# A two-block transformer kernel in fp32: raw first units, norm sums on TensorE, a shared convolution and new expert ends

## The reference

```
x = x + rms(conformer_conv(rms(x)*g));  x = x + rms(conv_ffn(rms(x)*g))   # first block
kv = rms(x) @ w_kv
x = x + rms(dilated_attention(rms(x)*g, kv)); x = x + rms(conv_ffn(...))  # second block
x = x + g1 * token_mixer(...)                 # mLSTM and differential attention
x = x + g2 * moe(...)                         # 32 experts, top 4 per token
return rms(x) * final_g
```

## Time and profile before

| | |
|---|---|
| median of 3 runs | 2433.94 us (2433.86, 2433.94, 2438.98) |
| profiled execution | 2438.93 us, span of the trace 2437.1 us |
| mean granted TensorE clock | 0.989 of full |
| busy: PE, DVE, ACT | 2360.7 (97%), 776.6 (32%), 424.8 us (17%) |
| read from HBM | 604.65 MB, 249 GB/s over the span |
| 192 expert loads | 2048 KB each, about 25 us from issue to landing |

### The profile page before, as it was taken

How to read it: one execution, slowest core, us unless ns; L and a number is a source line. 1 busy time by engine, 2 the same in 40 slices (tenths; PEclk the granted TensorE clock), 3 DMA queues, 4 the chain that set the end, 5 groups by cost and what they waited for, 6 DMA issues and landing times.

```text
span 2437.1 us, 31815 instructions
## 1 busy us (share of the span) xinstructions
PE 2360.7 (97%) x13140; PEld 1775.1 (73%) x13140; DVE 776.6 (32%) x1891; ACT 424.8 (17%) x1025; POOL 0.2 (0%) x4
## 2 busy tenths in 40 slices
PE   8899999999999999999999999999999999999997
PEld 7678887888888888988877787555555555555554
DVE  6843374310345422000344833222221111211122
ACT  3142202010142211100023502111111111111111
POOL 0000000000000000000000000000000000000000
PEclk9899999999999999899999999999999999999999
DMA  6124466665323443122122266999999999999995
GB/s 247 49 104 156 155 257 243 237 230 189 105 87 138 156 156 121 70 105 103 69 87 87 88 267 244 411 427 429 428 428 428 428 429 428 428 428 428 428 428 237
DMA packets 56631, 606.95 MB, mean 249 GB/s; under 512 B 6304, under 2 KB 6688, under 8 KB 7488
## 3 DMA queue, kind: packets, MB, share of 16 engines
q1 hardware_dynamic: 56544, 605.72, 62.1%
HBM read 604.65 MB, written 1.05 MB: 249 GB/s over the span
## 4 chain that ended last, share of the span: by engine, by line
PE 85%; DMA 7%; DVE 6%; issue 1%; ACT 1%; SPq 0%; DVEq 0%; ACTq 0%
PE bank L569 28%; PE bank L1067 17%; PE bank L566 8%; DMA ring<-in_experts 7%; PE bank L1093 6%; PE bank L632 5%; PE bank L583 3%; PE bank L1060 3%; PE bank L558 2%; DVE arena L1625 2%; PE bank L1028 2%; PE bank L1040 2%; PE bank L735 1%; PE bank L643 1%; PE bank L663 1%
## 5 line engine op out<-in xcount | busy, mean ns | idle before, releaser
L569 PE MATMUL bank<-arena,ring 128*128 128x256 f32 x3296 | 717.7, 380 | 0.0
L569 PEld LDWEIGHTS bank<-arena,ring 128*128 128x128 f32 x3296 | 627.6, 191 | 85.6
L2030 DVE TENSOR_SCALAR arena<-bank 128x256 f32<-128x256 f32 x64 | 27.2, 425 | 668.7 <-PE bank L1067 668.7
L1067 PE MATMUL bank<-ring,arena 128*64 128x256 f32 x2048 | 235.1, 382 | 4.8 <-DMA ring<-in_experts 4.8
L1067 PE MATMUL bank<-arena 128*64 128x256 f32 x2048 | 235.1, 382 | 2.1 <-DMA arena<-in_experts 2.1
L1067 PEld LDWEIGHTS bank<-ring,arena 128*64 128x64 f32 x2048 | 141.4, 137 | 91.3 <-issue 17.9
L1067 PEld LDWEIGHTS bank<-arena 128*64 128x64 f32 x2048 | 141.3, 137 | 88.4 <-issue 18.6
L566 PE MATMUL bank<-ring,arena 128*128 128x256 f32 x896 | 196.2, 381 | 0.0
L566 PEld LDWEIGHTS bank<-ring,arena 128*128 128x128 f32 x896 | 171.3, 191 | 23.5
L632 PE MATMUL bank<-arena,ring 128*128 128x256 f32 x576 | 124.6, 379 | 0.0
L632 PEld LDWEIGHTS bank<-arena,ring 128*128 128x128 f32 x576 | 109.4, 190 | 14.9
(11 more groups left out here) (270 smaller groups left out, 1959.4 us busy)
## 6 DMA issues: line engine op xcount, KB each, us to landing
arena<-in_experts SPq DMA_DIRECT2D x96, 2048.0 KB, 24.9
ring<-in_experts SPq DMA_DIRECT2D x96, 2048.0 KB, 26.5
ring<-in_dense SPq DMA_DIRECT2D x186, 1024.0 KB, 4.8
con<-in_con SPq DMA_DIRECT2D x1, 1248.0 KB, 12.2
X<-in_x SPq DMA_DIRECT2D x1, 1024.0 KB, 4.8
arena<-in_cond SPq DMA_DIRECT2D x1, 1024.0 KB, 17.6
arena<-in_ctx SPq DMA_DIRECT2D x1, 1024.0 KB, 4.8
arena<-in_mmask SPq DMA_DIRECT2D x1, 1024.0 KB, 6.8
```

What stands on the lines that cost most here:

```text
L569: ins = nc.tensor.matmul(o, w[:, k, j * P:(j + 1) * P], src[:, k, :], start=(k == 0), stop=(k == KT - 1))
L1067: ins = nc.tensor.matmul(o, XGT[:, k, e * CAP:(e + 1) * CAP], w[:, k, :], start=False, stop=(k == KT - 1), skip_group_check=True)
```

## The change

- **First two units.** ScalarE writes XG, X times the gain alone (in U's place), and units 0 and 1 multiply XG. The squares come after it; the sum (`presummed`) stands inside unit 0, before chunk 5. VectorE multiplies both halves of the two units by the factor as it reads PSUM (`raw_unit`), ScalarE takes the sigmoid in SBUF, and the gate adds the bias (`scalar_tensor_tensor`). Units 2 to 7 use H as before. SP loads X, 64 columns of gains, slab 0, and only then the constants and the other parameters.
- **Convolution.** The last 8 taps of channel 5 go to TensorE (`DIAG5`), and one addition joins the parts. The gates 4 to 7 lie between taps of channels 2 and 3. The channel means are added up as channels end; ScalarE, not VectorE, takes channels 6 and 7 out of PSUM.
- **Norms n1, n3, n6, n8.** VectorE adds squares 0 to 5 (`_part`); TensorE sums that and squares 6 and 7 in one group of three matmuls (`part_summed`). n10 likewise, with one-column matmuls (`token_sums`).
- **Experts.** One bias matmul of 512 columns serves two up steps. A pair starts when the first half of its tokens is there, and waits for the second before product 4 of step 0. The four increments stand ahead of the tables.
- **End.** The last scatter starts with half of YE. VectorE adds squares 0+1 and 2+3; the sum is taken by one-column matmuls, root and reciprocal are taken of 2 columns, and a diagonal matrix times ones spreads them back to 256 columns in PSUM, where the scaling reads them.

```diff
@@ sync
             sp.dma_start(X, d_x).then_inc(sem("x_in"), 16)
-            first = CON["upto"]
-            sp.dma_start(con[:, 0:first], d_con[:, 0:first]).then_inc(sem("con_in"), 16)
-            sp.dma_start(par[:, :], d_par).then_inc(sem("par_in"), 16)
+            first, gains = CON["upto"], PAR["cm_b_in"]
+            sp.dma_start(par[:, 0:gains], d_par[:, 0:gains]).then_inc(sem("gains_in"), 16)
...
+                if g == 1:
+                    sp.dma_start(con[:, 0:first], d_con[:, 0:first]).then_inc(sem("con_in"), 16)
+                    sp.dma_start(par[:, gains:NPAR], d_par[:, gains:NPAR]).then_inc(sem("par_in"), 16)
@@ tensor
+            def part_summed(name):
+                for n, c in enumerate((0, KT - 2, KT - 1)):
+                    if c:
+                        pe.wait_ge(sem(name + "_sq"), before(name + "_sq") + c + 1)
+                    else:
+                        pe.wait_ge(sem(name + "_part"), before(name + "_part") + KT - 3)
+                    ins = nc.tensor.matmul(banks[STAT][:, 0:T], mean, SQ[:, c, :], start=(n == 0), stop=(n == 2))
+                ins.then_inc(sem(name + "_sum"), 1)
...
-            pe.wait_ge(sem("con_in"), 16)
-            presummed("n0", 0)
-            stage("cm_in", H, "n0_h", busy=6)
+            pe.wait_ge(sem("x_in"), 16)
+            for _ in range(3):
+                nc.tensor.matmul(half_of(0, 1), X[:, 0, 0:P], X[:, 0, :], start=True, stop=True)
+            def first_chunk(k):
+                if k == 5:
+                    pe.wait_ge(sem("con_in"), 16)
+                    presummed("n0", 0)
+                pe.wait_ge(sem("n0_g"), k + 1)
+            product(FIRST_UNIT["cm_in"], SLAB_AT["cm_in", 0], XG, False, first_chunk)
+            stage("cm_in", XG, first=1, count=1)
+            stage("cm_in", H, "n0_h", first=2, count=6)
...
+            conv_taps(5, banks[WORK + 3][:, 0:T], TAPS - PE_TAPS, 0)
+            conv_taps(6, banks[WORK + 1][:, 0:T], 0, PE_TAPS)
+            for c in range(4):
+                channel_sum(c)
+            conv_taps(7, banks[WORK + 2][:, 0:T], 0, PE_TAPS + TAPS)
+            for c in range(4, KT):
+                ins = channel_sum(c)
...
+            def token_sums(name, c, first, last):
+                pe.wait_ge(sem(name + "_sq"), before(name + "_sq") + c + 1)
+                for t in range(2):
+                    ins = nc.tensor.matmul(banks[0][:, t:t + 1], SQ[:, c, t * P:(t + 1) * P], C("mean1024", 1),
+                                           start=(first and t == 0), stop=last, skip_group_check=True)
...
-            pe.wait_ge(sem("n10_presum"), before("n10_presum") + KT - 1)
-            for t in range(2):
-                ins = nc.tensor.matmul(banks[0][:, t:t + 1], SQ[:, 0, t * P:(t + 1) * P], C("mean1024", 1), start=True, stop=True)
+            pe.wait_ge(sem("n10_sq"), before("n10_sq") + 7)
+            pe.wait_ge(sem("n10_presum"), before("n10_presum") + 5)
+            token_sums("n10", 0, True, False)
+            token_sums("n10", 6, False, False)
+            token_sums("n10", 7, False, True)
...
@@ up
-                    nc.tensor.matmul(banks[i // 2 % 2][:, i % 2 * T:(i % 2 + 1) * T], ONEH, B1[:, i * T:(i + 1) * T],
+                        nc.tensor.matmul(banks[i // 2 % 2][:, :], ONEH, B1[:, i * T:(i + 2) * T],
...
+                        if i == 0 and k == 4:
+                            pe.wait_ge(sem("xgt"), n * 2 + 2)
@@ after the last pair
-            scatter(n_end)
-            pe.wait_ge(sem("scat_read"), n_end * 4 + 6)
-            stat("n11", 0, mean)
+            for j in range(4):
+                scatter(n_end, j, j + 1, ye_halves=1 + j // 2)
+            for i in range(2):
+                pe.wait_ge(sem("n11_pairs"), i + 1)
+                token_sums("n11", 2 * i, i == 0, False)
+            for c in range(4, KT):
+                token_sums("n11", c, False, c == KT - 1)
+            for _ in range(2):
+                nc.tensor.matmul(banks[2][:, 0:T], ident, C("ident", T), start=True, stop=True)
+            pe.wait_ge(sem("n11_diag"), 1)
+            nc.tensor.matmul(banks[1][:, 0:T], ones, NDIAG, start=True, stop=True).then_inc(sem("n11_wide"), 1)
@@ vector
+            raw_unit(0)
+            normed("n0", factor, lambda c: ("mix_pre", c))
+            dve.wait_ge(sem("par_in"), 16)
+            glu(0)
+            raw_unit(1)
+            glu(1)
+            conv(0)
+            glu(2)
+            glu(3)
+            conv(2, between={4: (4, 5), 14: (6,), 22: (7,)})
+            conv(4, own=(TAPS, TAPS - PE_TAPS))
             dve.wait_ge(sem("conv_pe"), 1)
+            V.tensor_tensor(U[:, 5, :], U[:, 5, :], banks[WORK + 3][:, 0:T], ALU.add).then_inc(sem("conv"), 1)
```

More of the change, by code:

```diff
@@ L737, in _ @@
-            ins.then_inc(sem("conv_pe"), 1)
-            for c in range(KT):
-                pe.wait_ge(sem("conv"), c + 1)
-                ins = nc.tensor.matmul(banks[WORK][:, 0:T], mean, U[:, c, :], start=(c == 0), stop=(c == KT - 1))
+            pe.wait_ge(sem("x_in"), 16)
[6 more added lines that the diff above has]
+                pe.wait_ge(sem("n0_g"), k + 1)
@@ new lines, in _, with conv_taps @@
+            product(FIRST_UNIT["cm_in"], SLAB_AT["cm_in", 0], XG, False, first_chunk)
+            stage("cm_in", XG, first=1, count=1)
+            stage("cm_in", H, "n0_h", first=2, count=6)
+            def conv_taps(c, o, first, at):
+                pe.wait_ge(sem("glu"), c + 1)
+                for k in range(first, TAPS):
+                    pe.wait_ge(sem("diag"), at + k - first + 1)
+                    w = DIAG[:, at + k - PE_TAPS, :] if at else DIAG5[:, k - first, :]
+                    ins = nc.tensor.matmul(o, w, G[:, c, k:k + T], start=(k == first), stop=(k == TAPS - 1))
+                ins.then_inc(sem("conv_pe"), 1)
@@ new lines, in channel_sum @@
+            def channel_sum(c):
+                if c < 6:
+                    pe.wait_ge(sem("conv"), c + 1)
+                else:
+                    pe.wait_ge(sem("conv_act"), c - 5)
+                return nc.tensor.matmul(banks[WORK][:, 0:T], mean, U[:, c, :], start=(c == 0), stop=(c == KT - 1))
+            conv_taps(5, banks[WORK + 3][:, 0:T], TAPS - PE_TAPS, 0)
+            conv_taps(6, banks[WORK + 1][:, 0:T], 0, PE_TAPS)
+            for c in range(4):
+                channel_sum(c)
@@ L1031, in gather, with scatter @@
                         ins.then_inc(sem("gathered"), 1)
-            def scatter(n, first=0, end=4):
-                pe.wait_ge(sem("ye"), n * 2 + 1)
+            def scatter(n, first=0, end=4, ye_halves=2):
+                pe.wait_ge(sem("ye"), n * 2 + (ye_halves - 1))
                 pe.wait_ge(sem("sgt"), n + 1)
@@ L1506, in residual, with presum @@
                          .then_inc(sem(name + "_x"), 1)
-            def presum(name, first=1, end=KT):
+            def presum(name, first=1, end=KT, to="_presum"):
                 for c in range(first, end):
@@ L2011, in add_scattered @@
                     ins.then_inc(sem("scat_read"), 1)
+                    if last and j in (1, 2):
+                        squares_paired(2 * j - 2)
             def body(p, odd):
```

136 lines of the change are left out of this document (84 added, 52 removed).

## The result

| | before | after |
|---|---|---|
| median | 2436.03 us (2433.86 to 2438.98, 4 runs) | 2407.18 us (2405.35 to 2410.87, 4 runs) |
| profiled execution | 2438.93 us, span 2437.1, clock 0.989 | 2408.92 us, span 2407.1, clock 0.994 |

The ratio is 0.9883, 95% interval 0.9863 to 0.9902: 28.9 us faster in the medians, 30.0 between the two profiled executions. The forecast was 2412.5, a gain of 21.5, with a range of 2406 to 2419. The time lies inside the range, 1.2 us from its lower end, and the gain is real, but it is 7.4 us larger than reckoned. Some 2 of these 7.4 are the median of the kernel before, which stood at 2433.94 in the three runs known to the forecast and at 2436.03 with the fourth. Most of what follows is about the rest.

The account below looks back on a forecast made before the run. TensorE (in the convolution also VectorE) sets the pace up to about 1500 us, then the expert weight stream; 14.8 + 2.1 + 0.9 + 0.8 + 0.4 + 2.5 = 21.5 off the median 2433.94 gives 2412.5, range 2406 to 2419.

Parts of the forecast that it names:

- Front, 14.8: Start of the kernel through convolution and channel means: last four means at 101.7 against 116.5 us, a gain of 14.8.
- The bound of 0.8: Front loads: the 32 KB of gains would hold slab 0 back by up to 0.8 us, the front gaining that much less.
- Norms, 2.1: Norms n1, n3, n6, n8: 0.55 us each at n1, n6, n8 and 0.49 at n3; 2.1 together, bounds 0 and 2.6.
- Router, loss 0.4: Router sum n10: 12 one-column instructions in place of 4 end at 1485.6 against 1485.1; a loss of 0.4 us.
- First pair, 0.9 net: First expert pair: earlier increments and half of the tokens start it 0.9 us earlier, router's loss included; bounds 0 and 1.4.
- Merged biases, 0.8 and 0.4: Expert up steps: 0.2 us per pair of steps, bounds 0 and 0.4; 0.8 ahead of the stream, 0.4 in the last pair.
- The end, 2.5: After the last pair: new sum gains 2.5 us (1.0 at low clock, upper bound 3.2); half of YE nothing, bound 0.6.
- number 1: Whole kernel: everything goes as worked out, own range 2408 to 2417; chance 0.62.
- Rival 2: Clock falls in TensorE's 2.5 us idle at 97.2 to 99.7, or most runs fall 5.0 higher: 2414.5 to 2418; chance 0.22.
- Rival 3: Expert part gives nothing, as the stream or first bias matmul starts by something else: 19.8 or 17.3 off, 2417; chance 0.07.
- 4: Front does not reach the end; only last pair and tail remain, 2.9 off: 2431, no change; chance 0.04.
- 5: Slower: TensorE falls to 1.2 GHz for the whole convolution and becomes its bound: 2442; chance 0.02.

## Why the prediction was right in its parts, and short in its sum

**Front, 14.8: right.** 14.86 at `cm_out`'s first product. Two sizes inside were off and cancelled. Unit 0 ended at 17.4, not 16.8, since TensorE's first 20 instructions took 6.14 us (they come 0.42 apart up to 11.5, not up to my 10.7, and 0.22 apart from 11.8), and the convolution started at 26.4, not 25.8. I had called this slow pace the low clock; the granted clock of these microseconds stands at 1.00 in the profile, in both kernels, so the rows show the pace and not its cause (busy us and count by engine, then granted clock, DMA share, GB/s):

```profile
8.00:12.00 4.00, 4.00 (x11) 3.00 (x10) 1.70 (x4) 3.70 (x12) 0.00 (x0) 1.00 1.06 437
```

The single steps of channel 4 cost 0.51 (52 steps in 21.54, of which 44 at 0.397), not 0.58; 4.1 for eight, between my 4.6 and the 3.2 that the page of the Trainium skill gave (VectorE: DVE Perf Modes, The DRAIN you can't avoid). The transfer of 32 KB did not hold slab 0 back: the gains were in use at 5.94 and the slab at 8.42, 0.2 after my time for it. The bound of 0.8 that I gave by the Trainium skill (DMA: Bandwidth & Descriptors, Bandwidth) did not come.

**Norms, 2.1: right.** 0.55 at n1 and n8 in the traces, and 0.55 again when undone.

**Router, loss 0.4: 0.25.** Undoing it showed this size, and that so small a change can be paid for elsewhere.

**First pair, 0.9 net: 1.1.** 1.35 for the increments and the half of the tokens, less 0.25.

**Merged biases, 0.8 and 0.4: mis-sized, 2.8.** This is the first step that was off. I priced the merge by the matmul alone: 0.62 twice against 1.05, 0.2 for a pair of steps. Steps of the last pair, before:

```profile
2378.93 0.69 PE L1060 MATMUL bank<-arena 32*128 32x256 f32 x2
2379.55 3.67 PE L1067 MATMUL bank<-arena 128*64 128x256 f32 x32
2383.16 0.69 PE L1060 MATMUL bank<-arena 32*128 32x256 f32 x2
```

and changed:

```profile
2355.13 1.12 PE L1109 MATMUL bank<-arena 32*128 32x512 f32 x2
2356.18 7.13 PE L1118 MATMUL bank<-arena 128*64 128x256 f32 x64
2363.24 1.12 PE L1109 MATMUL bank<-arena 32*128 32x512 f32 x2
```

A pair of steps takes 8.11 us instead of 8.46 (twice 4.23), so 0.35. Of this, what the matmul's own length does not give lies between the steps: 32 products followed by a bias take 3.61 from start to start of the next group, 64 in a row take 7.06, 0.16 less than twice that. My upper bound was 0.4, so the size of one merge was inside it. Four pairs of steps ahead of the gapless stream gave 1.4 (46.72 to 45.32 us from the first bias to the load), and bias to down fell from 904.5, 904.3 and 903.2 in the three profiles of the old code to between 901.2 and 902.3: 2.3 on the mean. Undone, the whole gave 3.4 on the mean of both kernels. I take 2.8. The steps themselves account for 2.1 of it, 1.4 up to that load and 0.7 in the last pair. The other 0.7 falls into the stream between that load and the last one that TensorE waits for, which took from 826.8 to 828.8 us over all fourteen profiles; that it belongs to the merge is not shown.

**The end, 2.5: right for the sum, but the place missed.** The new sum is worth 2.1 at the full clock, 2.5 in the medians when put in alone, and half of YE nothing. On top came 1.9 because the scatter no longer had to await a second block of code behind the loop. I had that stretch in the earlier trace rows, 3.19 us of issue, and wrote "not a wait on data". Then the prediction put its change at nothing. By the reading above that is the step that was missed: it was a wait on code, and any change of the number of instructions can remove it or bring it.

**The clock.** The first profile of before had the scatter at the low clock (2.5 us more than in the second), behind the idle stretch of 3.19. That is part of the 30.0 between the profiled executions. From the gates' first small matmul to the first unit of `mv` the kernel before took 33.7 us in its first profile and 30.3 in its second, the changed one 30.3 and 33.8: the clock comes back sooner or later behind small matmuls. The 3.4 us that the first pair of profiles shows there are a draw and no property of the change.

The sum with sizes as measured is 14.9 + 2.1 + 1.1 + 2.8 + 2.1 + 1.9 = 24.9. The means of all runs, 2434.4 (51) and 2407.3 (9), stand 27.0 apart. Of the remaining 2.1 I can name the low clock in the scatter, 2.5 us in one profile of before and 1.5 in the one with the new end, absent in the third and in both profiles of the changed kernel: 1.3 on the mean. 0.8 stays open. A difference of that size stands ahead of the expert loop: the first bias of the two profiles of the changed kernel stands 18.9 us before that of the three with the old code, on the means, and 18.1 are named.

**Rivals.** By its mechanism number 1 was the case, but the time, 2407.2, lies below its own range of 2408 to 2417 and inside the 2405 to 2408 to which the prediction had given a chance of 0.03 for more gain than reckoned. That the range as a whole held is in part the width left for other cases. Rival 2 was right that the clock can fall behind an idle stretch of 2 us, but not between 97.9 and 99.6, where it stayed at 1.00. Rival 3 is refuted by the undone steps, 4 and 5 by the trace.

## What to carry to other kernels

Price an instruction that is taken away by the distance between its neighbours in both patterns, not by its own length: what stands between two groups can cost more than its own length. That it is the change of shape was not tested. Look for idle time of TensorE of 2 us and for long runs of few-column matmuls before looking for microseconds elsewhere: eight more filler products here and a new order of 32 small ones were worth some 4 us. The spread of the runs went from 8 us to 0.5 in four runs with them, but was 6.5 in five runs of a kernel that has them too. When a kernel with a loop moves by 2 us and no dependency explains it, compare the "issue" behind the loop, the length of its branch and the count of instruction loads before believing in the edit.

## What the runs showed that was not expected

- **The clock after an idle stretch is a draw.** The changed kernel and its variants leave TensorE idle for some 2.1 us behind n1 and n6 and 2.3 to 2.4 ahead of `kv`. Nine profiles keep all three gaps; the low clock followed in four of them behind n1, in six ahead of `kv` and in seven behind n6. In the two with the gaps behind n1 and n6 filled it came nowhere of the three. A unit then takes 8.86 us instead of 7.17.
- **Small matmuls lower it each time.** 64 instructions of 16 columns in a row brought it to 0.55 or below in a stretch of 4 us in every profile that had them; in groups of 16 between units the clock stayed at 1.00 in both. In the first of these two it fell once more at 997.2, behind 40 instructions of four columns in a row, and in the second, with these in two groups, it did not.
- **Code loads behind a loop** make a jump of 3.4 to 3.8 us, of which TensorE's queued work hid all but 0.9 to 1.7; where the code falls across a block, some 2 more, and a stop can stand between two instructions of one line.
- **A step behind a step** is cheaper by 0.16 us, beside the length of the bias itself, when no bias matmul stands between.
